# Splitting weight units in pairs from the output projection on

## The chip, the cores and the metric

One core of a Trainium2 chip runs the whole program. The metric is the device time of one launch in microseconds. A core has TensorE (PE, matmul), ScalarE (ACT), VectorE (DVE), GpSimd (POOL) and SyncE (SP, here the issuer of the DMAs); each runs its own instruction stream in order, and they meet only at semaphores.

## The reference

One decoder layer on 544 tokens (512 of a prompt, 32 decode tokens), width 2048, all float32:

```
proj = rmsnorm(x) @ w_in                    # 2048 x 4096: pool part, q, k, v
mix  = concat(pooled, attention) @ w_out    # 2048 x 2048, the output projection
x    = x + rmsnorm(mix)
gt   = h @ w_gate ; up = h @ w_up           # 2048 x 5632 each, h = rmsnorm(x)
f    = gelu(causal depthwise conv3(gt)) * up
x    = x + rmsnorm(f @ w_down)              # 5632 x 2048
```

## The kernel before, in words

Every product is made of three passes in a 32-bit format of TensorE: a weight w is split into w_hi (a rounding copy) and w_lo = w - w_hi, an activation likewise, and w_hi*a_hi, w_hi*a_lo, w_lo*a_hi are added in PSUM. The weights come as *units* of 256 input rows by 256 output columns, 128 partitions x 512 numbers, 256 KB.

**The ring.** A unit passes through four steps. SP loads it into one of `RING = 4` slots of `w_raw` (`load_unit`, L363). ScalarE writes w_hi (`split_hi`, L371). VectorE writes w_lo (`split_lo`, L377). TensorE multiplies. Unit n uses slot n % 4 of all three buffers. A load waits until VectorE has split unit n-4 (`lo_ready`); ScalarE waits for the load (`w_loaded`, one semaphore a slot) and until TensorE is done with unit n-4 (`unit_used`); VectorE waits for ScalarE (`hi_ready`); TensorE waits for `lo_ready`. The order on ScalarE and VectorE is written out by hand: in the step in which TensorE is at unit k they split unit k + `LEAD`, LEAD = 3, and around that stands the rest of their work.

**The stages from the output projection on.**
- *First tile and halves.* The first output tile pair is made in the pool stage (q = Q_POOL). Then 14 token halves (`HALVES`) of 8 units each, b = 0 to 111 (L990): a unit multiplies only one half (272) of the tokens, 12 matmuls. After each group of 8, ScalarE squares and scales the result (`half_out`), VectorE adds squares (`add_half`). From b = 56 on, the first half of the tokens is finished beside it: every sixth step VectorE does `x2_pair` (L1672, L1675), ScalarE `x2_hi` (L755) and a step later `x2_squares` (L767), VectorE `x2_lo` (L1681) and `x2_add` (L1693).
- *Gate and up.* 44 feature tiles in 11 chunks of 4. A gate group is 8 units (`ff_unit`, L928) of 24 matmuls each. Its end is the *gate tail*: VectorE scales the gate and up tiles out of PSUM (L1735 to L1743), ScalarE starts the convolution (L791), VectorE does two taps (L1746, L1749), ScalarE the gelu (L794), VectorE the product (L1753), ScalarE the high part of f (`f_part`, L798), VectorE the low part (L1758). In `gate_group` on both engines the 8 splits stand first and the tail behind them, so the splits of the next group's step 0 stand behind the tail. Groups alternate between two sets of PSUM banks, and TensorE goes from one group to the next.
- *First chunk.* Groups 0 and 1 are interleaved (PAIR): units 0 to 3 as halves (`pair_halves`, L1005), then whole; splits at k = 1 to 15 alternate with the second half's x2_pair, x2_hi, x2_squares, x2_lo, x2_add. The tail of group 0 stands at k = 14, that of group 1 at u = 1 of the next group.
- *Down.* After four gate groups 4 x 4 units (L928 with f_hi, f_lo), which VectorE adds to `acc` (L1809). Units k = 0, 1 need tiles 0, 1 of f, units 2, 3 tiles 2, 3.
- *End.* The last down product (`end_unit`, L1263) runs in two column parts, 340 and 204; its units 4 to 15 are split into kept buffers over act_hi and act_lo (`end_projection`, L870, L1862).

Of the kernel before, what the change touches and what calls it, by code (L numbers as in the profile page):

```python
# [20 lines left out]
F32 = mybir.dt.float32  # L21
F32R = mybir.dt.float32r
ALU = mybir.AluOpType
# [20 lines left out]
CH = 4  # L44
# [12 lines left out]
RING = 4  # L57
# [102 lines left out]
def build(nc, xT, units, kcache, vcache, table, gains, pool_hist, conv_par, rope_tab, consts,  # L160
          yT, kT_out, vT_out, ext_out, tail_out):
    with ExitStack() as ctx:
# [202 lines left out]
        def split_hi(act, q, k, first=False):  # L365

            s = k % RING
            act.wait_ge(w_loaded[s], 16 * (q + k // RING + 1))
            if not first:
                act.wait_ge(unit_used, 4 * q + k - RING + 1)  # L370
            act.activation(w_hi[:, s], w_raw[:, s], ACT.Copy).then_inc(hi_ready, 1)  # L371

        def split_lo(dve, q, k):

            s = k % RING
            dve.wait_ge(hi_ready, 4 * q + k + 1)
            dve.tensor_tensor(w_lo[:, s], w_raw[:, s], w_hi[:, s].bitcast(F32), ALU.subtract).then_inc(lo_ready, 1)  # L377

        def tile_done(eng, G, mt, q, k):

# [117 lines left out]
        def _(act):  # L498
# [270 lines left out]
            first_out()  # L769
            for b in range(8 * HALVES):  # L770
                i, u = divmod(b, 8)
                split_hi(act, Q_HALF, b + LEAD)
                if u == 0 and i:
                    half_out(i - 1)
                b -= 56
                if b == 3:
                    root(2, 4)
                if b in FIRST_AT:
                    x2_hi(0, FIRST_AT[b])
                if b - 1 in FIRST_AT:  # L780
                    x2_squares(0, FIRST_AT[b - 1])
# [18 lines left out]
            def chunk(c, first=False, last=False):  # L800
                q0 = c * Q_CH + Q_FF
                g0 = c * G_CH + G_FF

                def gate_group(j, before=None):
                    for u in range(8):
                        split_hi(act, 2 * j + q0, u + LEAD)
                        if before is not None and u == 1:
                            ff_gate(g0 + before, before)
                            f_part(before, before)
                    F = c * CH + j  # L810
                    ff_gate(j + g0, F)
                    f_part(F, j)
                if first:
                    split_hi(act, q0, LEAD)
                    half_out(HALVES - 1)
                    root(3, 4)
                    x2_hi(1, 0)
                    x2_hi(1, 1)
                    x2_squares(1, 0)
                    x2_squares(1, 1)  # L820
                    x2_hi(1, 2)
                    for k in range(1, 16):
                        split_hi(act, q0, k + LEAD)
                        if k == 1:
                            x2_squares(1, 2)
                        if k in (2, 4, 6, 8, 10):
                            x2_hi(1, k // 2 + 2)
                        if k in (3, 5, 7, 9, 11):
                            x2_squares(1, k // 2 + 2)
                        if k == PAIR_END:  # L830
                            root(4)
                        if k == PAIR_END + 2:
                            ff_gate(g0, 0)
                            f_part(0, 0)

                    gate_group(2, before=1)
                    gate_group(3)
                else:
                    with act.Fori(0, CH) as j:
                        gate_group(j)  # L840
                if last:
                    return
                with act.Fori(0, 4) as d:
                    for k in range(4):
                        split_hi(act, d + q0 + 2 * CH, k + LEAD)

            def end_squares(g):

# [12 lines left out]
            def end_projection(q):  # L861

                for x in range(16):
                    if x + LEAD < RING:
                        split_hi(act, q, x + LEAD)
                    elif x + LEAD < 16:
                        k = x + LEAD
                        act.wait_ge(w_loaded[k % RING], 16 * (q + k // RING + 1))
                        act.wait_ge(unit_used, 4 * q)
                        act.activation(kept_hi[:, k - RING], w_raw[:, k % RING], ACT.Copy).then_inc(hi_ready, 1)  # L870
                    if x >= 4 and x % 4 >= 2:
                        end_squares(x // 4 * 2 + x % 4 - 4)
                for g in range(6, 16):
                    end_squares(g)
                    if g == 8:
                        root(5, 5)
                root(6, 3)
# [426 lines left out]
        def _(dve):  # L1304
# [389 lines left out]

            for b in range(8 * HALVES):
                i, u = divmod(b, 8)
                split_lo(dve, Q_HALF, b + LEAD)
                if b == 1:
                    add_first()
                if u == 1 and i:  # L1700
                    add_half(i - 1)
                b -= 56
                if b == 3:
                    mean_square(2, ps_b[0:TOK, 0, 0:4])
                if b == 4:
                    root_mean(2, 4)
                if b == 7:
                    rstd_half(0)
                    dve.wait_ge(x_again, 64)
                if b in FIRST_AT:  # L1710
                    x2_pair(0, FIRST_AT[b])
                if b - 2 in FIRST_AT:
                    x2_lo(0, FIRST_AT[b - 2])
                if b - 3 in FIRST_AT:
                    x2_add(0, FIRST_AT[b - 3])

            def gate_group(c, j, odd, pair=False):
                q = 2 * j + c * Q_CH + Q_FF + 2 * odd
                for u in range(8):
                    split_lo(dve, q, u + LEAD)  # L1720
                    if pair and u == 1:
                        gate_tail(c, 0, 1, c * Q_CH + Q_FF, 15)
                gate_tail(c, j, odd, q, 7)
# [37 lines left out]
            def chunk(c, first=False, last=False):  # L1761
                q0, g0 = c * Q_CH + Q_FF, c * G_CH + G_FF
                if first:
                    split_lo(dve, q0, LEAD)
                    add_half(HALVES - 1)
                    mean_square(3, ps[0:TOK, 0, 1, 0:4])
                    root_mean(3, 4)
                    rstd_half(1)
                    x2_pair(1, 0)
                    x2_lo(1, 0)  # L1770
                    x2_pair(1, 1)
                    x2_lo(1, 1)
                    x2_pair(1, 2)
                    for k in range(1, 16):
                        split_lo(dve, q0, k + LEAD)
                        if k in (1, 3, 5, 7, 9, 11):
                            x2_lo(1, k // 2 + 2)
                        if k in (2, 4, 6, 8, 10):
                            x2_pair(1, k // 2 + 2)
                        if k in ADD_AT:  # L1780
                            x2_add(1, ADD_AT.index(k))
                        if k == PAIR_END:
                            mean_square(4)
                        if k == PAIR_END + 1:
                            root_mean(4)
                            rstd_in(4)
                        if k == PAIR_END + 2:
                            gate_tail(c, 0, 0, q0, PAIR_END)

                    gate_group(c, 2, 0, pair=True)  # L1790
                    gate_group(c, 2, 1)
                else:
                    with dve.Fori(0, CH // 2) as j:
                        for odd in range(2):
                            gate_group(c, 2 * j, odd)

                def down(d, ahead):
                    for k in range(4):
                        if k < ahead:
                            split_lo(dve, d + q0 + 2 * CH, k + LEAD)  # L1800
                        if k >= 2:
                            for mt in range(2):
                                i, g = k - 2, 2 * d + g0 + CH + k - 2
# [50 lines left out]
            def end_projection(q):  # L1854

                for x in range(16):
                    if x + LEAD < RING:
                        split_lo(dve, q, x + LEAD)
                    elif x + LEAD < 16:
                        k = x + LEAD  # L1860
                        dve.wait_ge(hi_ready, 4 * q + k + 1)
                        dve.tensor_tensor(kept_lo[:, k - RING], w_raw[:, k % RING], kept_hi[:, k - RING].bitcast(F32),  # L1862
                                          ALU.subtract).then_inc(lo_ready, 1)
                    if x % 4 >= 2:
                        g = x // 4 * 2 + x % 4 - 2
                        end_evict(g)
                        if g >= 2:
                            end_add(g - 2)
# [234 lines left out]
```

## Time and profile before

| | us |
|---|---|
| median of 3 runs (lowest, highest) | 2462.1 (2461.23, 2463.46) |
| the profiled execution's own time | 2462.3 |
| its span | 2460.5 |
| PE busy | 2408.0 (98%) |
| DVE busy | 1145.7 (47%) |
| ACT busy | 746.5 (30%) |

The chain that ended last is 91% PE, 4% DVE, 2% DMA and 2% ACT. The granted clock of TensorE is 0.994 as a mean. A busy share tells how long an engine had work in flight; it does not tell whether a stage has room left, which is read from the order of events inside the stage. A bracket in a timeline row is the idle time of the engine before the row and what ended it; "x3" means three instructions merged in one row.

### The profile page before, as it was taken

The page shows a single profiled execution, that of the slowest core. Times are in us where ns is not written, and L with a number is a line of the kernel's source. Part 1 is how long each engine was busy: PE and PEld are TensorE (multiplying, and loading weights), DVE is VectorE, ACT ScalarE, POOL GpSimd, SP SyncE. Part 2 cuts the span into 40 slices and gives each one's busy share as a digit, 9 for nine tenths or more (in the row PEclk, how much of TensorE's full clock was granted, in tenths as well). Part 3 has the DMA queues.
Part 4 walks back from the last instruction along what each step waited for, and adds up shares of the span by engine and source line. Part 5 has one row for each costly group of instructions (what it writes and reads, how often), then busy time and mean ns, then how long its engine had stood idle before and what let it go on. Part 6 is the DMA issues. An engine that isn't in the chain of part 4 may idle for free.

```text
span 2460.5 us, 52956 instructions
## 1 busy us (share of the span) xinstructions
PE 2408.0 (98%) x20646; PEld 2331.9 (95%) x20646; DVE 1145.7 (47%) x1962; ACT 746.5 (30%) x1362; POOL 66.7 (3%) x235
## 2 busy tenths in 40 slices
PE   8999999999999999999999999999999999999996
PEld 8999988777999899999999999999999999999996
DVE  6634433346547754343444434344444443444347
ACT  5212322322455432222222222222222222222233
POOL 3000000000000000000000000000000000000000
PEclk9999999999999999999999999999999999999998
DMA  5499799997665323222232322222232322222232
GB/s 177 150 390 345 294 337 348 341 342 263 206 170 155 108 82 90 86 89 86 81 94 79 96 86 89 85 85 90 81 94 78 97 85 89 85 85 90 82 109 78
DMA packets 176374, 362.78 MB, mean 147 GB/s; under 512 B 19681, under 2 KB 23778, under 8 KB 175746
## 3 DMA queue, kind: packets, MB, share of 16 engines
q1 hardware_dynamic: 174178, 353.04, 44.1%
q0 software_dynamic: 2080, 8.14, 0.8%
q8 instruction: 80, 1.31, 0.2%
q14 instruction: 36, 0.29, 0.0%
HBM read 349.00 MB, written 12.10 MB: 147 GB/s over the span
## 4 chain that ended last, share of the span: by engine, by line
PE 91%; DVE 4%; DMA 2%; ACT 2%; DVEq 1%; issue 1%; SPq 0%; ACTq 0%
PE ps_acc L928 32%; PE ps_a L928 16%; PE ps_b L928 16%; PE ps_acc L905 13%; PE ps_acc L990 4%; PE ps_a L1126 2%; PE ps_a L1054 2%; DMA w_raw<-units 1%; DVE w_lo L377 1%; PE ps_b L1095 1%; PE ps_a L905 1%; PE ps_b L905 1%; ACT w_hi L371 1%; PE ps_acc L1263 1%; DVE region L1852 0%
## 5 line engine op out<-in xcount | busy, mean ns | idle before, releaser
L377 DVE TENSOR_TENSOR w_lo<-w_raw,w_hi 128x512 fp32r<-128x512 f32 x768 | 525.3, 695 | 890.2 <-ACT w_hi L371 886.4
L371 ACT ACTIVATE w_hi<-w_raw 128x512 fp32r<-128x512 f32 x768 | 472.0, 628 | 1058.7 <-PE ps_acc L928 460.0
L928 PE MATMUL ps_acc<-act_hi,w_hi 128*128 128x272 f32 x1456 | 302.9, 290 | 12.9 <-DVE act_lo L1345 8.3
L928 PE MATMUL ps_acc<-act_lo,w_hi 128*128 128x272 f32 x1456 | 302.5, 289 | 0.0
L928 PE MATMUL ps_acc<-act_hi,w_lo 128*128 128x272 f32 x1456 | 300.8, 288 | 0.0
L928 PEld LDWEIGHTS ps_acc<-act_hi,w_hi 128*128 128x128 f32 x1456 | 229.2, 189 | 13.5 <-DVE w_lo L377 13.5
L928 PEld LDWEIGHTS ps_acc<-act_hi,w_lo 128*128 128x128 f32 x1456 | 230.0, 189 | 0.0
L928 PEld LDWEIGHTS ps_acc<-act_lo,w_hi 128*128 128x128 f32 x1456 | 229.6, 189 | 0.0
L905 PE MATMUL ps_acc<-act_hi,w_hi 128*128 128x272 f32 x832 | 180.3, 298 | 1.8 <-DVE scratch L1356 1.3
L905 PE MATMUL ps_acc<-act_hi,w_lo 128*128 128x272 f32 x832 | 172.4, 289 | 0.0
L905 PE MATMUL ps_acc<-act_lo,w_hi 128*128 128x272 f32 x832 | 172.1, 288 | 0.0
L928 PE MATMUL ps_a<-act_hi,w_hi 128*128 128x272 f32 x728 | 151.9, 290 | 0.0
L928 PE MATMUL ps_b<-act_lo,w_hi 128*128 128x272 f32 x728 | 151.0, 288 | 0.0
L928 PE MATMUL ps_a<-act_lo,w_hi 128*128 128x272 f32 x728 | 150.7, 288 | 0.0
L928 PE MATMUL ps_b<-act_hi,w_lo 128*128 128x272 f32 x728 | 150.3, 288 | 0.0
L928 PE MATMUL ps_b<-act_hi,w_hi 128*128 128x272 f32 x728 | 150.0, 288 | 0.0
L928 PE MATMUL ps_a<-act_hi,w_lo 128*128 128x272 f32 x728 | 149.6, 286 | 0.0
L905 PEld LDWEIGHTS ps_acc<-act_hi,w_hi 128*128 128x128 f32 x832 | 130.1, 190 | 13.3 <-issue 9.2
L990 PE MATMUL ps_acc<-act_hi,w_hi 128*128 128x272 f32 x448 | 130.1, 290 | 3.7 <-DVE w_lo L377 3.5
L928 PE MATMUL ps_acc<-f_hi,w_hi 128*128 128x272 f32 x640 | 132.3, 288 | 0.0
L928 PE MATMUL ps_acc<-f_lo,w_hi 128*128 128x272 f32 x640 | 132.1, 288 | 0.0
L928 PE MATMUL ps_acc<-f_hi,w_lo 128*128 128x272 f32 x640 | 131.8, 288 | 0.0
(309 smaller groups left out, 4302.2 us busy)
## 6 DMA issues: line engine op xcount, KB each, us to landing
w_raw<-units SPq DMA_DIRECT2D x780, 256.0 KB, 2.7
region<-kcache SPq DMA_DIRECT2D x128, 512.0 KB, 6.4
region<-vcache SPq DMA_DIRECT2D x256, 256.0 KB, 5.7
region<-xT SPq DMA_DIRECT2D x8, 544.0 KB, 6.7
region<-xT SPq DMA_DIRECT2D x4, 1088.0 KB, 8.6
yT<-region SPq DMA_DIRECT2D x8, 340.0 KB, 2.4
ext_out<-region POOLq DMA_DIRECT2D x8, 339.5 KB, 7.6
kT_out<-scratch POOLq DMA_DIRECT2D x8, 272.0 KB, 6.5
```

Source lines behind the costliest of these rows:

```text
L371: act.activation(w_hi[:, s], w_raw[:, s], ACT.Copy).then_inc(hi_ready, 1)
L377: dve.tensor_tensor(w_lo[:, s], w_raw[:, s], w_hi[:, s].bitcast(F32), ALU.subtract).then_inc(lo_ready, 1)
L905: mm = pe.matmul(banks(mt, odd)[:, n, 0:HN], w[:, s, i, cols], half(a[:, kt], n), start=kt == 0 and w is w_hi and a is hi, stop=kt == 2 * ...
L928: mm = pe.matmul(banks(mt, odd)[:, n, 0:HN], w[:, s, i, cols], half(a[:, kt], n), start=kt == 0 and w is w_hi and a is hi, stop=kt == 2 * ...
L990: mm = pe.matmul(ps[:, i % 2, mt, 0:HN], w[:, u % RING, j, mt * P:(mt + 1) * P], half(a[:, kt], i // 7), start=kt == 0 and w is w_hi and a ...
L1054: mm = pe.matmul(ps_a[quad * HC:(quad + 1) * HC, 0, r * P:(r + 1) * P], q_blk[:, h * HC:(h + 1) * HC], pages[:, slot, h * P:(h + 1) * P], ...
L1095: mm = pe.matmul(ps_b[:, 1, 0:P], v_toks[h // 2 % 2][:, h % 2, kj], probT[:, kj * P:(kj + 1) * P], start=kj == 0, stop=kj == qi)
L1126: mm = pe.matmul(ps_a[q * HC:(q + 1) * HC, 0 if f == 2 else 1, :], s_all[:, 4 * i + q, c:c + HC], halves[:, 4 * (turn % 4) + q, :], start= ...
L1263: mm = pe.matmul(out[:, mt], w[:, kt % 2, mt * P:(mt + 1) * P], a[:, kt, cols], start=kt == 0 and w is hi and a is f_hi, stop=kt == 3 and ...
```

## The change

From the output projection on, ScalarE and VectorE split two units with one instruction each. The pair (k, k+1), k even, is split in the step of unit k-2. It waits for both loads, and for `unit_used` to show that unit k-3 is done (both old units of the two slots). The counters rise by 2 when the pair is done. Loads stay one DMA a unit, each waiting for `lo_ready` as before. RING stays 4, so the ring holds two pairs. TensorE's program and SP's are untouched; so is everything up to and with the pool stage, LEAD = 3 there included. At the seam the halves' b = 0 splits one unit (LEAD), and pairs follow from b = 2 on. In the first chunk the pair 2, 3 stands where unit 3 stood, and pairs follow at even k.

```diff
+        def split_hi2(act, q, k):
+            s = k % RING
+            for i in range(2):
+                act.wait_ge(w_loaded[s + i], 16 * (q + k // RING + 1))
+            act.wait_ge(unit_used, 4 * q + k - RING + 2)
+            act.activation(w_hi[:, s:s + 2], w_raw[:, s:s + 2], ACT.Copy).then_inc(hi_ready, 2)
+
+        def split_lo2(dve, q, k):
+            s = k % RING
+            dve.wait_ge(hi_ready, 4 * q + k + 2)
+            dve.tensor_tensor(w_lo[:, s:s + 2], w_raw[:, s:s + 2], w_hi[:, s:s + 2].bitcast(F32),
+                              ALU.subtract).then_inc(lo_ready, 2)
...
             for b in range(8 * HALVES):
                 i, u = divmod(b, 8)
-                split_hi(act, Q_HALF, b + LEAD)
+                if b == 0:
+                    split_hi(act, Q_HALF, LEAD)
+                elif b % 2 == 0:
+                    split_hi2(act, Q_HALF, b + 2)
...
                 def gate_group(j, before=None):
                     for u in range(8):
-                        split_hi(act, 2 * j + q0, u + LEAD)
+                        if u % 2 == 0:
+                            split_hi2(act, 2 * j + q0, u + 2)
...
                 if first:
-                    split_hi(act, q0, LEAD)
+                    split_hi2(act, q0, 2)
                     half_out(HALVES - 1)
...
                     for k in range(1, 16):
-                        split_hi(act, q0, k + LEAD)
+                        if k % 2 == 0:
+                            split_hi2(act, q0, k + 2)
...
                 with act.Fori(0, 4) as d:
-                    for k in range(4):
-                        split_hi(act, d + q0 + 2 * CH, k + LEAD)
+                    for k in (0, 2):
+                        split_hi2(act, d + q0 + 2 * CH, k + 2)
...
                 for x in range(16):
...
+                    k = x + 2
+                    if x == 0:
+                        split_hi2(act, q, 2)
+                    elif x % 2 == 0 and k < 16:
+                        for i in range(2):
+                            act.wait_ge(w_loaded[k % RING + i], 16 * (q + k // RING + 1))
                         act.wait_ge(unit_used, 4 * q)
-                        act.activation(kept_hi[:, k - RING], w_raw[:, k % RING], ACT.Copy).then_inc(hi_ready, 1)
+                        act.activation(kept_hi[:, k - RING:k - RING + 2], w_raw[:, k % RING:k % RING + 2],
+                                       ACT.Copy).then_inc(hi_ready, 2)
```

VectorE's loops change in the same way, with `split_lo2`.

## Rows read from the trace of the kernel before

**Rows 1.** The page, part 1: busy time and share of each engine.

```profile
PE 2408.0 (98%) x20646; PEld 2331.9 (95%) x20646; DVE 1145.7 (47%) x1962; ACT 746.5 (30%) x1362; POOL 66.7 (3%) x235
```

**Rows 2.** The page, part 5: the low split; busy, mean ns, idle before.

```profile
L377 DVE TENSOR_TENSOR w_lo<-w_raw,w_hi 128x512 fp32r<-128x512 f32 x768 | 525.3, 695 | 890.2 <-ACT w_hi L371 886.4
```

**Rows 3.** Groups by line and shape: same operations, 1024 wide.

```profile
L655 ACT ACTIVATE f_hi<-region 128x1024 fp32r<-128x1024 f32 x4 | 4.2, 1053 | 2.2 <-DVE region L1557 2.2
L1569 DVE TENSOR_TENSOR f_lo<-region,f_hi 128x1024 fp32r<-128x1024 f32 x4 | 4.9, 1222 | 0.8 <-ACT f_hi L657 0.8
```

**Rows 4.** Windows, gate and down stages: length, then PE, PEld, DVE, ACT, POOL busy.

```profile
1250.00:1450.00 200.00, 200.00 (x1597) 200.00 (x1597) 84.31 (x135) 51.38 (x82) 3.09 (x20) 1.00 0.29 86
```

**Rows 5.** Timeline of PE: first matmul after a gate group's last.

```profile
1007.08 0.42 PE L928 MATMUL ps_a<-act_hi,w_hi 128*128 128x272 f32 x2
```

**Rows 6.** Timeline of ACT: start, length; end of that tail and next splits.

```profile
1012.18 0.66 ACT L798 ACTIVATE f_hi<-scratch 128x544 f32 x1 [0.96 <-DVE scratch L1754]
1012.75 1.66 ACT L371 ACTIVATE w_hi<-w_raw 128x512 fp32r<-128x512 f32 x3
1016.32 0.63 ACT L371 ACTIVATE w_hi<-w_raw 128x512 fp32r<-128x512 f32 x1 [1.91 <-PE ps_b L928]
```

**Rows 7.** Timeline of DVE: end of the same tail.

```profile
1013.00 0.72 DVE L1758 TENSOR_TENSOR f_lo<-scratch,f_hi 128x544 f32 x1 [0.95 <-ACT f_hi L798]
1013.64 1.89 DVE L377 TENSOR_TENSOR w_lo<-w_raw,w_hi 128x512 fp32r<-128x512 f32 x3
```

**Rows 8.** Timeline of PE in the end stage: restart after a wait.

```profile
2386.03 0.42 PE L1263 MATMUL ps_acc<-f_hi,w_hi 128*128 128x340 f32 x1 [1.81 <-DVE f_lo L1758]
2386.29 0.32 PE L1263 MATMUL ps_acc<-f_lo,w_hi 128*128 128x340 f32 x1
```

**Rows 9.** Timelines of ACT and DVE there.

```profile
2384.99 0.61 ACT L371 ACTIVATE w_hi<-w_raw 128x512 fp32r<-128x512 f32 x1
...
2385.25 0.72 DVE L1758 TENSOR_TENSOR f_lo<-scratch,f_hi 128x544 f32 x1 [0.96 <-ACT f_hi L798]
```

**Rows 10.** Windows: PE, PEld, DVE, ACT, POOL busy, then granted clock, DMA, GB/s.

```profile
836.00:840.00 4.00, 4.00 (x23) 4.00 (x23) 2.28 (x4) 3.09 (x7) 0.00 (x0) 0.63 0.00 0
...
2380.00:2390.00 10.00, 8.19 (x52) 7.91 (x52) 7.63 (x12) 4.97 (x9) 0.73 (x3) 1.00 0.33 117
```

**Rows 11.** Timeline of PEld: the wait ahead of the slow window.

```profile
834.16 0.19 PEld L1005 LDWEIGHTS ps_acc<-act_hi,w_hi 128*128 128x128 f32 x1 [3.53 <-issue]
```

**Rows 12.** Timelines of ACT, then DVE, in the halves past b = 56.

```profile
778.04 0.94 ACT L755 ACTIVATE act_hi<-region,gain 128x272 fp32r<-128x272 f32 x2 [2.71 <-DVE region L1675]
...
779.41 0.64 ACT L767 ACTIVATE scratch<-region 128x544 f32<-128x544 f32 x1
779.96 1.66 ACT L371 ACTIVATE w_hi<-w_raw 128x512 fp32r<-128x512 f32 x3
...
775.88 0.69 DVE L377 TENSOR_TENSOR w_lo<-w_raw,w_hi 128x512 fp32r<-128x512 f32 x1
...
777.28 0.73 DVE L1675 TENSOR_TENSOR region<-region 128x544 f32<-128x544 f32 x1
```

**Rows 13.** Waits of PEld, 735 to 826 us: total, times, longest.

```profile
PEld ps_acc L990 <- DVE w_lo L377: 3.7, 6, 1.6
```

**Rows 14.** Timelines at the start of the halves: PEld, then ACT.

```profile
650.39 0.19 PEld L990 LDWEIGHTS ps_acc<-act_hi,w_hi 128*128 128x128 f32 x1 [1.46 <-DVE w_lo L377]
...
650.85 1.92 ACT L371 ACTIVATE w_hi<-w_raw 128x512 fp32r<-128x512 f32 x3 [1.25 <-DMA w_raw<-units]
```

**Rows 15.** Timeline of ACT in the first chunk.

```profile
838.88 0.94 ACT L755 ACTIVATE act_hi<-region,gain 128x272 fp32r<-128x272 f32 x2 [0.91 <-DVE region L1675]
842.27 0.66 ACT L767 ACTIVATE scratch<-region 128x544 f32<-128x544 f32 x1 [1.94 <-DVE shared L1690]
```

**Rows 16.** DMA, one load issued at 1014.9, one at 671: issues, size, landing us.

```profile
w_raw<-units SPq DMA_DIRECT2D x1, 256.0 KB, 3.7
w_raw<-units SPq DMA_DIRECT2D x1, 256.0 KB, 2.6
```

More of the change, by code:

```diff
@@ L863, in end_projection @@
                 for x in range(16):
[L864 to L868, printed above, removed]
+                    k = x + 2
[4 more added lines that the diff above has]
+                            act.wait_ge(w_loaded[k % RING + i], 16 * (q + k // RING + 1))
                         act.wait_ge(unit_used, 4 * q)
-                        act.activation(kept_hi[:, k - RING], w_raw[:, k % RING], ACT.Copy).then_inc(hi_ready, 1)
+                        act.activation(kept_hi[:, k - RING:k - RING + 2], w_raw[:, k % RING:k % RING + 2],
+                                       ACT.Copy).then_inc(hi_ready, 2)
                     if x >= 4 and x % 4 >= 2:
@@ L1696, in _ @@
                 i, u = divmod(b, 8)
-                split_lo(dve, Q_HALF, b + LEAD)
+                if b == 0:
+                    split_lo(dve, Q_HALF, LEAD)
+                elif b % 2 == 0:
+                    split_lo2(dve, Q_HALF, b + 2)
                 if b == 1:
@@ L1719, in gate_group @@
                 for u in range(8):
-                    split_lo(dve, q, u + LEAD)
+                    if u % 2 == 0:
+                        split_lo2(dve, q, u + 2)
                     if pair and u == 1:
@@ L1763, in chunk @@
                 if first:
-                    split_lo(dve, q0, LEAD)
+                    split_lo2(dve, q0, 2)
                     add_half(HALVES - 1)
@@ L1774, in chunk @@
                     for k in range(1, 16):
-                        split_lo(dve, q0, k + LEAD)
+                        if k % 2 == 0:
+                            split_lo2(dve, q0, k + 2)
                         if k in (1, 3, 5, 7, 9, 11):
@@ L1798, in down @@
                     for k in range(4):
-                        if k < ahead:
-                            split_lo(dve, d + q0 + 2 * CH, k + LEAD)
+                        if k < ahead and k % 2 == 0:
+                            split_lo2(dve, d + q0 + 2 * CH, k + 2)
                         if k >= 2:
@@ L1856, in end_projection @@
                 for x in range(16):
[L1857 to L1863, printed above, removed]
+                    k = x + 2
+                    if x == 0:
+                        split_lo2(dve, q, 2)
+                    elif x % 2 == 0 and k < 16:
+                        dve.wait_ge(hi_ready, 4 * q + k + 2)
+                        dve.tensor_tensor(kept_lo[:, k - RING:k - RING + 2], w_raw[:, k % RING:k % RING + 2],
+                                          kept_hi[:, k - RING:k - RING + 2].bitcast(F32), ALU.subtract).then_inc(lo_ready, 2)
                     if x % 4 >= 2:
```

## The prediction

> **What bounds the kernel now.** I read the busy shares first: PE 98%, DVE 47%, ACT 30% [rows 1]. Then the windows: in the gate and down stages PE does 1597 matmuls in 200 us without idle time [rows 4], so a matmul costs 0.1252 us, a unit of 24 of them 3.01 us and a token-half unit of 12 1.50 us. The kernel is TensorE's stream. The two splitting engines wait most of the time (VectorE idles 890 us before its splits, for ScalarE [rows 2]), so making them cheaper can give nothing there. What counts is whether a unit is still ready in time; for that I read the timelines around a gate tail, the one place where both engines are away from the ring for several us.
>
> **How far ahead the ring is.** Before, when TensorE leaves a gate group it has three units ready (the step of unit 7 split unit 10); the next split, unit 11, stands behind the tail. After, the last pair ahead of the tail is (8, 9) and the next, (10, 11), stands behind it. So two units, 6.02 us, cover the tail instead of three, 9.03 us, and what comes behind it is a double split, done only when both halves are.
>
> **The gate tail, worked out.** A group ends and the next begins at 1007.08 [rows 5]. ScalarE's last tail step is f_part, 1012.18 to 1012.84; its next split starts at 1012.75 [rows 6]. VectorE's last tail step ends at 1013.72 [rows 7].
> - Now: the first of three low splits starts at 1013.64 and ends some 0.69 later at 1014.33 [rows 2, 7]; it is needed at 1007.08 + 9.03 = 1016.11. It is 1.8 us early: no stall.
> - After: the high split of 1024 columns starts at 1012.75. Its duration is shown by the same operation on 1024 columns: 1.053 us on ScalarE and 1.222 us on VectorE [rows 3]. High part until 1013.80; VectorE is free by then; it follows 0.03 later, until 1015.05. A restart of PE costs a little: after the wait in the end stage the first matmul began 0.06 us after the end of the instruction waited for (2385.97 to 2386.03), and the second came 0.26 behind it, where the steady pitch there is 0.157, so 0.16 us [rows 8, 9]. Unit 10 effectively starts at 1015.21; it is needed at 1007.08 + 6.02 = 1013.10. Stall: 2.1 us.
> Nothing gives this back: TensorE is the bound and has lost the time. It doesn't grow either: the pair (12, 13) is split right behind (10, 11), some 4 us before it is needed.
>
> This happens at every group whose tail stands between two ordinary pairs: groups 2 and 3 of the first chunk, four groups in each of nine chunks, three of the last: 2 + 36 + 3 = 41. Behind the fourth group of a chunk come down units; the third and fourth need f tile 3 in any case, but that ends at 1013.72 in this frame, before the weights. 41 x 2.1 = 86 us.
>
> Bounds of one stall: if the pair cost no more than a single split (0.63 + 0.69 [rows 2, 6]) the stall would be about 1.15 us; if it cost twice both single durations (1.26 + 1.39), 2.5 us. The measured 1024-wide rows are nearest; I take 2.1 and hold 1.9 to 2.35 likely.
>
> **Steady steps without a tail.** A high split starts 0.2 us after its unit boundary (1016.32 against 1016.11 [rows 6]). Pair: 0.2 + 1.05 + 0.03 + 1.22 + 0.16 = 2.66 us from the moment unit k-3 is done. Two whole units are 6.02: hidden by 3.4 us, down steps included (VectorE's two adds come behind it and have the rest). Two token-half units are 3.01: hidden by only 0.35 us.
>
> **Token halves, b = 56 to 111.** Every sixth step the chain x2_pair, x2_hi, x2_squares stands between two pair splits. From the boundary T: low split done at 2.50; x2_pair ends 1.44 after the low split (775.88 + 0.69 = 776.57 to 778.01); ScalarE, which is in order, waits for it and runs x2_hi from 3.97, 0.94 less 0.09 overlap, then x2_squares with a pitch of 0.55 (779.41 to 779.96) [rows 12]. The next high split starts at 5.4, ends 6.4, low 7.7, PE restarts at 7.85; needed at 6.02. 1.8 us, 8 times, and where half_out falls behind the late split, 0.5 us twice: 15.6 us. The waits there now are 3.7 us, with the 0.06 of each restart and 1.3 us at the seams around it some 5.4 [rows 13]; these vanish into the new ones. Net +10 us. With lead 3 the same chain had one unit more of room.
>
> **Start of the halves.** Units 4 and 5 are late already, because four large loads of x stand ahead of them: unit 4 starts at 650.4, and unit 5's high split at 650.85, when its load has landed [rows 14]. As a pair both wait for the second load: 650.85 + 1.05 + 0.03 + 1.22 + 0.16 = 653.3. Unit 6 then starts at 656.3 instead of about 653.8: +2.5 us.
>
> **First chunk.** The pair 2, 3 ahead of half_out delays it by 1.05 - 0.63 = 0.42 us, and the norm's chain with it, on which TensorE waits: +0.4. Then unit 4's split moves from k = 1 to k = 2, behind x2_squares. x2_hi ends at 839.82, x2_lo and the copy of x2_add (VectorE, some 1.3 us) and x2_squares (0.55 pitch, before at 842.27) [rows 15] let the pair start at 841.75; done at 844.2 against 841.7 now: +2.3 to 2.5. The tail of group 1 stands behind pair (18, 19) with units up to 19 ready, and by the same steps unit 20 is 1.8 us late. Together +4.6.
>
> **End.** Pair (2, 3) starts at 2384.99 [rows 9]: 2386.04, 2387.29, restart 2387.45, whole unit 2 still ahead, whereas at 2386.03 its first half (0.94) was done: +2.4.
>
> **The loads.** Both loads of a pair start when its old pair is split, 0.33 us apart on SP. In the gate stages they have 6 us and more. In the halves they have 2 x 3.01 + 0.2 - 2.50 = 3.7 us. Lone loads land in 2.6, the second of three issued 0.6 apart in 3.7 us [rows 16]. So a pair takes 2.95 (the lone one and the second issue) to 4.2 (0.5 of issue and 3.7). I take 3.5, no stall; at 4.2 it is 0.5 us each 4 units in the first 56 units, 7 us, and 0.8 us in each of 8 later rounds: 14 us in all.
>
> **Sum.** 86 + 10 + 2.5 + 4.6 + 2.4 = 105.5 us. On the profiled execution, 2462.3 us (span 2460.5 and 1.8 around it, 0.2 above the median), that gives 2568 us.
>
> **The skill against the change.** With these gaps the clock has to be asked for. After a wait of 3.53 us [rows 11] the granted clock of the window 836 to 840 was 0.63 (23 matmuls in 4 us, that is partly 1.2 GHz), and about 1.5 us were lost beyond the wait; after the wait of 1.81 us in the end stage the window stayed at 1.00 [rows 8, 10]. The Trainium skill ("TensorE: Matmul & The Clock Gate", Part 1) says that the clock is gated down once the array has been idle and comes back after sustained work; this trace agrees in both directions. By that rule, applied to each of the new gaps, the time is the one of rival 1.
>
> **Rivals.**
> 1. *Each gap lowers the clock.* New waits of 1.8 to 2.1 us lie between the 1.81 that did not and the 3.53 that did, nearer the first. If each of the 43 large ones cost 1.5 us more: 2568 + 65 = 2633 us. It decides only if the gap comes out well above 2.1.
> 2. *Late pairs of loads in the halves*, as bounded above: 2582 us. For it: the landing of 3.7 us. Against: in the halves a pair is issued alone.
> 3. *The tail is covered after all*, because ScalarE or VectorE reaches the pair earlier than their order says or the tail shortens by 2.1 us. Then 86 us fall away: 2482 us. Against it: the rows show the split starting only behind f_part.
> 4. *Not slower: the instruction count decides.* Place: the x2 rounds in the halves, where 5.4 us are lost now because VectorE is nearly full. The Trainium skill ("VectorE: DVE Perf Modes", the section on the TRN2 errata) says that operations from SBUF pay a fixed cost per instruction, so wide ones are better. The trace agrees on the size: 2 x 0.695 against 1.222 [rows 2, 3]. But back to back three singles take 1.89 [rows 7], 0.6 each, and two of those are the pair's 1.22: no gain where VectorE is full. If it gained all 5.4 us and the tail were covered: 2457 us. It decides from the point where a pair is ready within 6.02 us of the group's end; I find 8.1.
>
> **Chances.** Forecast 0.75, rival 1 0.06, rival 2 0.13, rival 3 0.03, rival 4 0.03. The forecast's own range, 41 x 1.9 to 41 x 2.35 and the rest 12 to 26 us, is 2552 to 2585; with the loads up to 2599. Range 2550 to 2600. The measurement can tell 0.2% (5 us) from no change: slower 0.96, same 0.02, faster 0.02.
>
> **What would show it.** In the changed profile TensorE's waits on the low split at L928 should total about 80 us in some 41 pieces of near 2 us, each about 6 us after a group's start, with a ScalarE instruction of 1.05 and a VectorE one of 1.22 just ahead. Halves: 8 waits of about 1.7 us past b = 56 and nearly none before but at the start. Granted clock in the gate stages 1.00. A gap of less than 1 us behind the tails, or waits on loads in the gate stages, would make the forecast wrong.

## The result and the profile after

| kernel | median us | lowest to highest | runs |
|---|---|---|---|
| before | 2463.46 | 2461.23 to 2467.17 | 5 |
| changed | 2620.93 | 2615.68 to 2625.84 | 5 |

The changed kernel is slower: ratio 1.0636, 95% interval [1.0624, 1.0648]. 2568 was forecast, with a range of 2550 to 2600; the direction was right, the time lies outside the range. The profiled execution of the changed kernel took 2619.86 us with a span of 2618.1, 157.6 above the span before.

The page, parts 1 and 5, of the changed kernel, against [rows 1 to 3]:

```profile
PE 2468.0 (94%) x20646; PEld 2382.2 (91%) x20646; DVE 1111.7 (42%) x1644; ACT 693.5 (26%) x1044; POOL 67.0 (3%) x235
...
L391 DVE TENSOR_TENSOR w_lo<-w_raw,w_hi 128x1024 fp32r<-128x1024 f32 x312 | 378.5, 1224 | 803.1 <-ACT w_hi L385 802.6
L385 ACT ACTIVATE w_hi<-w_raw 128x1024 fp32r<-128x1024 f32 x312 | 325.4, 1056 | 1026.9 <-PE ps_b L950 644.0
```

Both splitting engines do less (VectorE 34 us, ScalarE 53 us) and the kernel is 158 us longer. The pairs cost 1.056 and 1.224 us, as [rows 3] had it. PE's busy time grew by 60 us for the same 20646 matmuls, which the waits don't explain: its matmuls became slower.

Who TensorE waited for, in total us, times, longest, changed kernel:

```profile
PE ps_acc L950 <- DVE w_lo L391: 40.8, 22, 2.0
PE ps_a L950 <- DVE w_lo L391: 40.4, 21, 2.0
PE ps_acc L1012 <- DVE w_lo L391: 22.3, 13, 4.1
...
PE ps_acc L1285 <- DVE w_lo L391: 4.1, 1, 4.1
```

L950 is L928 of before (gate and down), L1012 is L990 (halves), L1285 is L1263 (end). In gate and down 43 waits make 81.2 us, where before there was none for a weight. One of them, with the engines before it (ACT, then DVE, then PE):

```profile
1042.34 0.66 ACT L816 ACTIVATE f_hi<-scratch 128x544 f32 x1 [0.96 <-DVE scratch L1780]
1042.97 2.00 ACT L385 ACTIVATE w_hi<-w_raw 128x1024 fp32r<-128x1024 f32 x2
```

```profile
1043.15 0.73 DVE L1784 TENSOR_TENSOR f_lo<-scratch,f_hi 128x544 f32 x1 [0.95 <-ACT f_hi L816]
1044.13 2.36 DVE L391 TENSOR_TENSOR w_lo<-w_raw,w_hi 128x1024 fp32r<-128x1024 f32 x2 [0.25 <-ACT w_hi L385]
```

```profile
1045.41 0.57 PE L950 MATMUL ps_a<-act_hi,w_hi 128*128 128x272 f32 x2 [1.99 <-DVE w_lo L391]
1045.78 0.66 PE L950 MATMUL ps_a<-act_lo,w_hi 128*128 128x272 f32 x2
1046.23 0.65 PE L950 MATMUL ps_a<-act_hi,w_lo 128*128 128x272 f32 x2
```

The pair starts at 1042.97, behind f_part; its low half follows 1.16 us later, TensorE 1.28 us after that. This is the forecast's chain, step for step, with the same 2 us at its end. What it did not have is in the last two rows: they start 0.45 us apart with two matmuls each, so the pitch behind this gap is 0.23 us, not 0.125. Windows of the changed kernel behind two gaps of the same length, 1.95 and 1.96 us (length, PE, PEld, DVE, ACT, POOL busy, granted clock, DMA, GB/s):

```profile
1074.00:1078.00 4.00, 4.00 (x34) 4.00 (x33) 0.33 (x1) 0.00 (x0) 0.00 (x0) 1.00 0.79 261
1100.00:1104.00 4.00, 4.00 (x22) 4.00 (x22) 0.66 (x1) 0.00 (x0) 0.00 (x0) 0.57 0.77 222
```

Behind one gap (1071.3 to 1073.2) the clock stays at 2.4 GHz, behind the other (1097.6 to 1099.6) it drops to the lower level, 1.2 GHz, for 3.4 us; 34 matmuls against 22. I call this a *fall*. In the changed kernel all last 3.4 us, so each loses 1.7 us. Between 640 us and 2590 us there are 33 in the changed kernel, 56.3 us in all, where before there was one. 26 of them lie past 900 us, 25 behind gaps and one behind the one-column sums of the first chunk.

The account of the 157.6 us: waits in gate and down +81.2; in the halves 22.3 - 3.5 = +18.8; in the end 4.1 - 1.8 = +2.3; the clock 56.3 - 1.7 = +54.6; the waits for act_lo in the first chunk, 4.6 us before, are gone. That makes 152.3; the rest, 5 us, is about what 0.1 us for each of some 50 restarts gives (an estimate from [rows 8], where the second matmul comes 0.1 us late). Without the clock: 103 us, where the forecast's sum had 105.5.

### The profile page after: what moved, and what is told of

It is laid out like the page before. It is cut to its first block, busy times and chain, and to the rows that moved or that the text cites. A ratio compares the mean times of both kernels' runs of the same rounds, so it can differ in the third digit from the quotient of the medians.

```text
span 2618.1 us, 52637 instructions
## 1 busy us (share of the span) xinstructions
PE 2468.0 (94%) x20646; PEld 2382.2 (91%) x20646; DVE 1111.7 (42%) x1644; ACT 693.5 (26%) x1044; POOL 67.0 (3%) x235
## 4 chain that ended last, share of the span: by engine, by line
PE 77%; DVE 10%; ACT 6%; DMA 2%; issue 2%; DVEq 2%; ACTq 1%; SPq 0%; POOL 0%; POOLq 0%
PE ps_acc L950 27%; PE ps_a L950 13%; PE ps_acc L927 12%; PE ps_b L950 12%; DVE w_lo L391 3%; PE ps_acc L1012 3%; ACT w_hi L385 3%; PE ps_a L1148 2%; PE ps_a L1076 2%; DMA w_raw<-units 2%; ACT scratch L809 1%; DVE scratch L1775 1%; DVE scratch L1772 1%; DVE scratch L1779 1%; ACT scratch L812 1%
## 5 line engine op out<-in xcount | busy, mean ns | idle before, releaser
L391 DVE TENSOR_TENSOR w_lo<-w_raw,w_hi 128x1024 fp32r<-128x1024 f32 x312 | 378.5, 1224 | 803.1 <-ACT w_hi L385 802.6
L385 ACT ACTIVATE w_hi<-w_raw 128x1024 fp32r<-128x1024 f32 x312 | 325.4, 1056 | 1026.9 <-PE ps_b L950 644.0
L950 PE MATMUL ps_acc<-act_hi,w_hi 128*128 128x272 f32 x1456 | 308.8, 294 | 29.4 <-DVE w_lo L391 21.3
L950 PE MATMUL ps_acc<-act_lo,w_hi 128*128 128x272 f32 x1456 | 306.9, 292 | 0.0
L950 PE MATMUL ps_acc<-act_hi,w_lo 128*128 128x272 f32 x1456 | 305.3, 291 | 0.0
L950 PEld LDWEIGHTS ps_acc<-act_hi,w_hi 128*128 128x128 f32 x1456 | 233.8, 193 | 32.0 <-DVE w_lo L391 23.9
L950 PEld LDWEIGHTS ps_acc<-act_lo,w_hi 128*128 128x128 f32 x1456 | 234.4, 193 | 0.0
L950 PEld LDWEIGHTS ps_acc<-act_hi,w_lo 128*128 128x128 f32 x1456 | 234.3, 192 | 0.0
L950 PE MATMUL ps_a<-act_hi,w_hi 128*128 128x272 f32 x728 | 157.9, 299 | 40.4 <-DVE w_lo L391 40.4
L927 PE MATMUL ps_acc<-act_hi,w_hi 128*128 128x272 f32 x832 | 180.4, 298 | 1.8 <-DVE scratch L1378 1.3
L377 DVE TENSOR_TENSOR w_lo<-w_raw,w_hi 128x512 fp32r<-128x512 f32 x144 | 103.4, 725 | 173.5 <-ACT w_hi L371 172.5
L950 PEld LDWEIGHTS ps_a<-act_hi,w_hi 128*128 128x128 f32 x728 | 118.1, 194 | 45.0 <-DVE w_lo L391 45.0
L950 PE MATMUL ps_acc<-f_hi,w_hi 128*128 128x272 f32 x640 | 137.1, 297 | 19.5 <-DVE w_lo L391 19.5
L1012 PE MATMUL ps_acc<-act_hi,w_hi 128*128 128x272 f32 x448 | 134.1, 299 | 22.4 <-DVE w_lo L391 22.3
L950 PE MATMUL ps_a<-act_lo,w_hi 128*128 128x272 f32 x728 | 155.0, 295 | 0.0
L950 PE MATMUL ps_b<-act_lo,w_hi 128*128 128x272 f32 x728 | 154.0, 293 | 0.0
L950 PE MATMUL ps_a<-act_hi,w_lo 128*128 128x272 f32 x728 | 153.9, 293 | 0.0
L950 PE MATMUL ps_b<-act_hi,w_hi 128*128 128x272 f32 x728 | 153.7, 293 | 0.0
L950 PE MATMUL ps_b<-act_hi,w_lo 128*128 128x272 f32 x728 | 153.2, 292 | 0.0
```

Of the source, the lines that this page charges most:

```text
L385: act.activation(w_hi[:, s:s + 2], w_raw[:, s:s + 2], ACT.Copy).then_inc(hi_ready, 2)
L391: dve.tensor_tensor(w_lo[:, s:s + 2], w_raw[:, s:s + 2], w_hi[:, s:s + 2].bitcast(F32), ALU.subtract).then_inc(lo_ready, 2)
L927: mm = pe.matmul(banks(mt, odd)[:, n, 0:HN], w[:, s, i, cols], half(a[:, kt], n), start=kt == 0 and w is w_hi and a is hi, stop=kt == 2 * ...
L950: mm = pe.matmul(banks(mt, odd)[:, n, 0:HN], w[:, s, i, cols], half(a[:, kt], n), start=kt == 0 and w is w_hi and a is hi, stop=kt == 2 * ...
L1012: mm = pe.matmul(ps[:, i % 2, mt, 0:HN], w[:, u % RING, j, mt * P:(mt + 1) * P], half(a[:, kt], i // 7), start=kt == 0 and w is w_hi and a ...
```

## The experiments

Each was timed beside the kernel before on the same chip; the ratio is to that. "Hit" are the gaps past 900 us (waits of TensorE of over 0.5 us) with a fall at them.

| kernel | median us | ratio, interval | most gaps behind a tail | hit / gaps |
|---|---|---|---|---|
| changed | 2620.9 | 1.0636 [1.0624, 1.0648] | 1.86 to 2.01, twice 1.4 | 25 / 42 |
| e1 | 2488.0 | 1.0097 [1.0080, 1.0114] | none | 0 / 1 |
| e2 | 2592.7 | 1.0520 [1.0503, 1.0538] | 1.94 to 2.09 | 22 / 42 |
| e3 | 2512.6 | 1.0194 [1.0177, 1.0211] | 1.08 to 1.22 | 1 / 41 |
| e4 | 2604.5 | 1.0566 [1.0548, 1.0584] | 0.2 and 1.86 to 2.01 | 17 / 21 |
| e5 | 2462.6 | 0.9989 [0.9980, 0.9999] | none | 0 / 2 |
| e6 | 2546.0 | 1.0335 [1.0319, 1.0351] | 1.34 to 1.49 | 2 / 42 |
| e7 | 2622.0 | 1.0641 [1.0625, 1.0657] | 2.38 to 2.48 | 16 / 42 |
| e8 | 2641.7 | 1.0721 [1.0704, 1.0739] | 2.89 to 3.00 | 12 / 42 |
| e9 | 2554.2 | 1.0364 [1.0347, 1.0381] | 1.56 to 1.71 | 2 / 42 |
| e10 | 2616.7 | 1.0616 [1.0595, 1.0637] | 1.86 to 2.01 | 25 / 42 |

**e1, pairs in the halves alone; e2, pairs behind them alone.**

```diff
 e1, from the kernel before
-                split_hi(act, Q_HALF, b + LEAD)
+                if b == 0:
+                    split_hi(act, Q_HALF, LEAD)
+                elif b % 2 == 0:
+                    split_hi2(act, Q_HALF, b + 2)
...
-                    split_hi(act, q0, LEAD)
+                    split_hi2(act, q0, 2)
 e2, from the changed kernel: the same places the other way round; VectorE alike
```

> Pairs only in the token halves and for units 2, 3 of the first chunk; from k = 1 of the first chunk on single splits with lead 3. Theory (lead lost at long chains, plus a TensorE clock that falls after some of the gaps): no waits on the low split of about 2 us in the gate stages and a granted clock of 1.00 there; in the halves nine waits, 8 x 1.8 and 4.1 at the start, and four or five clock falls of 1.7 us each; about 25 us above before, 2483 to 2492. Rival (the clock has no part): 14 to 17 us above before.

> Single splits in the halves, pairs from k = 2 of the first chunk on. Theory: 43 waits of 2.0 us at L950-like lines as in the changed kernel (81 us) and some 26 clock falls of 1.7 us (44 us), so 2463 + about 133 = 2590 to 2602; the two parts of the change add up to the whole within some 5 us. Rival (the clock has no part): 2463 + 90 = 2553.

Measured: e1 +23.5 us, e2 +128.2 us, together 151.7; the whole change was 157.5 in its first timing and 152.0 in that of e10. Both times came out where the theory had them. For e2 the rival without the clock is off by 40 us. e1 says little of the clock: of the four or five falls expected there were three, one of them 6.8 us long, together 5 us more than before, and the waits alone grew by more (19.3 us) than the rival's 14 to 17. TensorE's waits in e1, halves:

```profile
PE ps_acc L1008 <- DVE w_lo L391: 22.8, 15, 4.2
...
PE ps_acc L946 <- DVE act_lo L1699: 4.6, 3, 2.7
```

Before, the waits at that line were 3.5 us. Five sixths of the loss is made behind the halves.

**e3, the lead of 2 with single instructions.** The lines that these replace are left out.

```diff
         def split_hi2(act, q, k):
+            for i in range(2):
+                split_hi(act, q, k + i)
         def split_lo2(dve, q, k):
+            for i in range(2):
+                split_lo(dve, q, k + i)
```

> At the places of the pairs two single instructions on each engine, each with its own wait, so the lead of 2 stays and the double width goes (the kept units of the end stay pairs). Theory (the wait is lead plus width): unit 10 is ready at 14.33 + 0.16 in the frame of the gate tail, so the waits are 1.3 to 1.4 us instead of 2.0, 41 x 1.35 = 56 us; in the halves 0.9 instead of 1.8. If gaps of 1.4 us leave the clock alone: 2463 + 56 + 10 = about 2530. If they lower it as often as the 2.0 us ones do (33 falls of 1.7): 2585. Rival (the width alone is to blame, not the lead): no waits behind the tails, 2465.

Waits of TensorE between 1200 and 2300 us:

```profile
PE ps_acc L945 <- DVE w_lo L377: 17.8, 15, 1.2
PE ps_a L945 <- DVE w_lo L377: 16.2, 15, 1.1
```

The waits are 1.1 to 1.2 us, shorter than my 1.35, and one gap is hit past 900 us, the 3.35 us wait of the end stage. The time is 17 us under the expected 2530, because in the halves the waits didn't grow at all (3.3 us in total, 3.5 before) where 10 us were expected. So behind the tails the shorter lead costs some 48 us by itself, nearly all of it waits; the double width adds 0.85 us to each wait, and only then the clock falls behind the tails. In the halves the whole loss comes with making the pair one instruction, that is with its width and its wait for both loads; which of the two weighs more no run shows.

**e4, half of the gaps filled.**

```diff
+            def fill(G, odd):
+                pe.wait_ge(acc_free, 2 * G)
+                for _ in range(8):
+                    pe.matmul(banks(0, 1 - odd)[:, 0, 272:400], ident, ones, start=True, stop=True)
...
                 for u in range(8):
+                    if odd and u == 2:
+                        fill(G, odd)
```

> The changed kernel, with 8 extra float32 matmuls of ident and ones (128 columns, into a PSUM bank that is free then; they add nothing to the result) ahead of the wait at unit 2 of every odd gate group. So 21 of the 41 gaps are mostly filled with work that is done while TensorE would wait, 20 stay empty. Theory (a gap of 2 us without work lowers the clock in some of its occurrences): no clock fall behind a filled gap, falls behind the empty ones as before; about 11 to 14 falls fewer, 2621 - 20 = 2597 to 2605, if the 8 matmuls fit into 2 us. Rival (the falls have another cause than the idle time, say the restart itself or a schedule of their own): as many falls as before, 2621.

One of the filled gaps:

```profile
1092.52 1.95 PE L1240 MATMUL ps_acc<-cst 128*128 128x128 f32 x16
...
1094.64 0.52 PE L950 MATMUL ps_a<-act_hi,w_hi 128*128 128x272 f32 x2 [0.17 <-DVE w_lo L391]
```

Behind the 21 filled gaps there is no fall, in the changed kernel 11 of these had one. Of the 21 left empty 17 are hit. That makes 8 hits fewer, not the 11 to 14 expected, since 3 more of the empty gaps are hit than in the changed kernel. The kernel is 16.5 us faster (12 against e10) though TensorE does 336 extra instructions. The falls come from the idle time.

**e5, the pair moved into the tail.** From e2, with single splits in the halves. The chain of the tail has holes: ScalarE waits 2.0 us between L791 and L794, so the pair fits there. The row of the kernel before:

```profile
1010.55 0.67 ACT L794 ACTIVATE scratch<-scratch 128x560 f32<-128x560 f32 x1 [2.00 <-DVE scratch L1749]
```

Excerpts of the edit:

```diff
 ScalarE, ff_gate
                     .then_inc(c_started, 1)
+                if ahead is not None:
+                    split_hi2(act, ahead, 10)
                 act.wait_ge(c_ready, F + 1)
 VectorE, gate_tail
                                          ALU.mult, ALU.add).then_inc(c_ready, 1)
+                if ahead:
+                    split_lo2(dve, q, 10)
                 dve.wait_ge(gelu_done, F + 1)
 and the pair of step 0 goes from gate_group, down and end_projection
```

> Pairs from k = 2 of the first chunk on, singles in the halves, and the pair that stood behind each gate tail stands inside it: on ScalarE between the start of the convolution and the gelu (2.0 us idle there), on VectorE between the second tap and the product. Theory (the whole loss of the FFN part is that the pair (10, 11) stood behind the tail): unit 10 is ready 11.8 us into the frame where it is needed at 13.1, no waits of 2 us, granted clock 1.00, and only the first chunk's entry costs 1 to 4 us: 2463 to 2468. Rival (pairs as such are too coarse for the ring, whatever their place): waits of 0.5 to 1 us stay behind the tails, 2485 to 2520.

ACT and DVE of e5 in a tail, then a window over ten chunks of it:

```profile
1008.24 1.04 ACT L385 ACTIVATE w_hi<-w_raw 128x1024 fp32r<-128x1024 f32 x1
1010.71 0.68 ACT L811 ACTIVATE scratch<-scratch 128x560 f32<-128x560 f32 x1 [1.43 <-DVE scratch L1769]
```

```profile
1010.59 1.22 DVE L391 TENSOR_TENSOR w_lo<-w_raw,w_hi 128x1024 fp32r<-128x1024 f32 x1
1011.73 0.69 DVE L1775 TENSOR_TENSOR scratch<-scratch 128x512 f32<-128x512 f32 x1
```

```profile
1200.00:2300.00 1100.00, 1100.00 (x8776) 1100.00 (x8775) 448.76 (x578) 256.33 (x273) 33.27 (x120) 1.00 0.28 87
```

TensorE has no idle time and does the same 8776 matmuls as before in that stretch; the changed kernel does 8076. In the gate and down stages pairs as such are harmless; their place behind the tail was the loss. For the halves e5 shows nothing, since it has singles there. e5 is 0.1% faster than before, with an interval that ends just under 1, and 0.4 us under the expected 2463 to 2468: it beats the changed kernel by 6% and the kernel before by next to nothing. In the first chunk the 4.6 us of waits for act_lo are gone, but from 640 us to the end stage its trace has 10.2 us at the lower clock against 3.4 before, which takes 3.4 us back.

**e6 to e9, the length of the gap.** e6: the low split as two single instructions behind the double high one. e7: one ScalarE copy of 512 columns, of no use, ahead of the pair. e8: two of them. e9: e6 with a copy of 256.

```diff
 e6
+            for i in range(2):
+                dve.tensor_tensor(w_lo[:, s + i], w_raw[:, s + i], w_hi[:, s + i].bitcast(F32),
+                                  ALU.subtract).then_inc(lo_ready, 1)
 e7, e8 (second line in e8 alone)
                     f_part(F, j)
+                    act.activation(conv[:, 2:2 + SEQ], f_buf[:, 0:SEQ], ACT.Copy)
+                    act.activation(probT, f_buf[:, 0:SEQ], ACT.Copy)
```

> The changed kernel with the high split double and the low split as two single instructions behind it. Unit 10 is ready 0.5 us sooner, so the 41 waits are 1.5 us instead of 2.0 (60 us). The clock: 2.0 us gaps lowered it in about six cases of ten, 1.1 us ones never. If what counts is the length of the gap, 1.5 us lie between and few or no falls follow: 2463 + 60 + 18 = 2541 with none, 2560 with a third of them. Rival (it falls at any gap that comes from a pair's schedule): 25 falls, 2584.

> The changed kernel with one more ScalarE copy of 512 columns (of f_buf, into a buffer that is dead there) ahead of the pair behind each ordinary tail: the gap grows by 0.55 us to 2.5. Theory (the chance of a fall grows with the length of the gap): 41 x 0.55 = 23 us from the waits, and falls behind eight or nine of ten gaps instead of six: 8 to 14 more of 1.7 us: 2621 + 23 + 19 = 2655 to 2670. Rival (a fall has a fixed chance per gap): 2644.

> As e7_gap_longer with a second extra copy of 512 columns (into another dead buffer): gaps near 2.9 us. e7 had gaps of 2.4 us and 16 falls behind 42 of them, fewer than the changed kernel's 25 behind 2.0 us. Theory A (the chance of a fall grows with the gap): falls behind nearly all 42 gaps; waits 41 x 0.9 = 37 us over the changed kernel, clock about +15 us, 2670. Theory B (above a length between 1.5 and 2.0 us, whether a gap lowers the clock depends on where in time it lies, and its chance hardly on its length; a fall that begins inside the gap costs less than 1.7 us): 15 to 28 falls, 2640 to 2660.

> As e6_double_hi_single_lo (gaps of 1.34 to 1.49 us, 2 falls in 42) with one extra ScalarE copy of 256 columns ahead of the split behind the tail: gaps of about 1.75 us. Theory A (the chance grows steadily from 1.5 to 2.0 us): 10 to 15 falls; 2546 + 13 + 20 = about 2580. Theory B (a sharp step above 1.9 us): 2 or 3 falls, 2559.

Waits between 1200 and 2300 us: e9, e7, e8.

```profile
PE ps_a L952 <- DVE w_lo L392: 25.4, 15, 1.7
PE ps_acc L952 <- DVE w_lo L392: 24.1, 15, 1.7
```

```profile
PE ps_acc L951 <- DVE w_lo L391: 34.0, 14, 2.5
PE ps_a L951 <- DVE w_lo L391: 33.5, 14, 2.4
```

```profile
PE ps_acc L952 <- DVE w_lo L391: 41.3, 14, 3.0
PE ps_a L952 <- DVE w_lo L391: 40.7, 14, 2.9
```

Up to 1.71 us no gap past 900 us is hit. The two hits of e6 and of e9 are one long wait in the end stage (3.5, 3.8 us) and the first gap behind the first chunk, which is longer than its fellows, 1.76 and 1.97 us. So the shortest gap with a fall past 900 us is e6's of 1.76. Of the changed kernel's 39 gaps of 1.86 to 2.01 us 24 are hit. My expectation for e7 was wrong: fewer of the longer gaps are hit (16, then 12), so 19 us more of waits left the median at the changed kernel's (2622.0). Theory A of e8 and of e9 falls with it. Theory B was right for e9 and in kind for e8, though with fewer hits than its 15. For e6 the guess of "none or few" held, 2546.

**e10, the changed kernel once more.**

> The changed kernel itself, for a second trace. If the falls depend on where the gaps lie against something that runs on its own, their number differs from the 26 past 900 us of the first trace by a few and they stand behind other gaps, and the time moves by some 1.7 us a fall within 2616 to 2626; if they hang on the gaps' own lengths, the same gaps are hit again.

25 gaps hit again, the same but for one (the gap near 1359 us has none, that near 1387 has one). This repeat does not decide between the two readings, since gaps and falls lie alike in it, both about 0.6 us earlier (gap 1042.9 and fall 1045.1 against 1043.4 and 1045.7). That the hits came again is luck, as far as is known.

The length of a gap doesn't decide either: within the changed kernel it is the same for hit and unhit ones. The clock records of the traces, which give the start of each fall, do.

In each trace all falls, whatever gap they follow, start at times of one evenly spaced series, to 0.01 us (in the changed kernel 1045.73, 1100.34, 1127.65, 1230.05 and so on). Where this series lies differs between two traces of the same kernel, by 0.7 us between the changed kernel and e10, so the program alone does not set it. Of the 39 gaps of 1.86 to 2.01 us past 900 us, the 24 hit ones have no time of the series inside them, or one at most 0.06 us from an end; each of the 15 others is cut by one at least 0.13 us from both ends. The gaps behind tails of e10 and e2 and the empty ones of e4 part in the same way (at most 0.09 us when hit, at least 0.12 when not, the 1.4 us ones apart). In e7 and e8 the gaps of 2.4 and 2.9 us that are hit are those cut nearer to an end, the unhit ones those cut nearer to their middle, without an exception. So whether a gap of some 2 us lowers the clock is decided by its place against something that runs beside the kernel. This is read from the traces; no run moved a gap to test it.

## Why the prediction was wrong

- *The lead and the tail: right.* 41 waits of 2.1 us were forecast, 86 us; behind the tails there are 41, two of 1.4 us in the first chunk and 39 of 1.86 to 2.01, plus 0.1 of restart each. e3 and e5 show the two causes apart: lead, and place behind the tail.
- *The halves: right in kind.* Waits of 1.8 us at the x2 rounds and 4.1 at the start; the total rose by 18.8 where 10 + 2.5 was forecast. Three waits of 0.6 to 1.5 us between 673 and 725 us, 3.3 us together, were not in the sum. They are rival 2, late loads, on a small scale: the loads ahead of them took 4.2, 4.8 and 4.8 us to land (issued at 666.5, 700.7 and 717.6), and ScalarE's split starts 0.2 to 0.4 us after each of these landings and TensorE 2.4 us after the split's start. No run took this apart. And the waits before were 3.5 us at that line, not the 5.4 I subtracted.
- *First chunk: wrong in sign.* +4.6 was forecast. The wait at unit 4 came (1.76 us), that at unit 20 did not, and the 4.6 us of waits for act_lo, which I had not looked at, vanished.
- *End: right* (+2.3, forecast +2.4).
- *The sum without the clock: luck in part.* 103 against 105.5 us looks close, but the halves were 6 us too low and the first chunk 7 us too high, and these two cancel.
- *The step that failed: the clock.* The prediction put rival 1 at 6%, because a wait of 1.81 us had left the clock alone and one of 3.53 had not, took "nearer the first" as safe, and wrote that it decides only if the gap comes out well above 2.1. It came out at 2.0 and 25 of 42 gaps lowered the clock. With the halves there are 33 falls, 54.6 us more than before, where the sum had nothing; rival 1, applied to all 43 gaps, had 65. One unhit gap [rows 10] proves nothing where only some are hit: the same 1.95 us is hit or unhit within the changed kernel, and that gap of before, 2384.2 to 2386.0, is cut 0.8 us from its end by a time of its trace's series. The Trainium skill ("TensorE: Matmul & The Clock Gate", Part 1), which says that the clock falls after idleness, was the right warning in kind, and 24 of the 39 gaps of 1.86 to 2.01 us agree; I gave it too little weight. e3 against the changed kernel and e4 show the cause: shorter or filled gaps, no falls behind them.

Open: what sets the series of times at which falls start, and whether moving the gaps against it would avoid the falls. In e7 and e8 most gaps lie so that a time of the series cuts them near the middle, which is why the longer gaps were hit less often there; other places would give other counts.

## What to carry to other kernels

A ring's lead is used up where its feeders do something long; count what stands ready when they leave and what stands behind them in their order, in the consumer's time. Widening an instruction that is off the critical path saves nothing and halves the ring's grain; if it is done, put it into a hole of the long chain, not behind it. In this kernel a wait of TensorE of 2 us cost its length plus, in 24 cases of 39, 1.7 us of lowered clock; price the clock before calling such a wait small, and don't take one gap without a fall as proof.

## What was not expected of the hardware

- Past 900 us, gaps of 1.76 us and more lowered TensorE's clock in some cases (24 of 39 at 1.86 to 2.01 us in the changed kernel), gaps up to 1.71 us in none. A fall lasted 3.4 us and cost 1.7; in e1, e2, e4, e5, e7, e8 and e10 one or two lasted 6.8.
- Longer gaps were not hit more often: 25, 16 and 12 of 42 in the kernels with gaps of 2.0, 2.4 and 2.9 us.
- All falls of a trace start at times of one evenly spaced series, whose place differs from trace to trace; a gap of about 2 us that lies between two of its times is hit, one that is cut by such a time by more than 0.1 us is not.
- Float32 matmuls of no use during the wait kept the clock up: 0 falls behind 21 gaps.
